# A recurrent unit's gate products as three fp32r passes, with inputs and weights split channel by channel

## The reference, cut to what matters

```python
def rg_lru(u, w_rg, b_rg, w_ig, b_ig, lru_lambda):
    ...
    ub = uf.reshape(B, S, LRU_BLOCKS, LRU_BLOCK_DIM)
    r = jax.nn.sigmoid(jnp.einsum('bshi,hij->bshj', ub, w_rg).reshape(B, S, LRU_WIDTH) + b_rg)
    i = jax.nn.sigmoid(jnp.einsum('bshi,hij->bshj', ub, w_ig).reshape(B, S, LRU_WIDTH) + b_ig)
    ...
    log_a = -LRU_C * r * jax.nn.softplus(-lru_lambda)
    a = jnp.exp(log_a)
    xin = jnp.sqrt(-jnp.expm1(2.0 * log_a)) * (i * uf)
    ...
    _, h = lax.associative_scan(combine, (a, xin), axis=1)
```

## Time and profile before

| | us |
|---|---|
| median of 3 runs | 2747.89 |
| lowest, highest | 2747.36, 2748.41 |
| the profiled execution, its own time | 2748.5 |
| span of that execution | 2746.7 |
| TensorE busy in it | 2711.8 (99%) |
| ScalarE, VectorE, GpSimd busy | 1533.2, 1812.7, 1052.8 |
| mean granted TensorE clock | 0.998 |

### The profile page before, as it was taken

How to read it: one execution, slowest core, us unless ns; L and a number is a source line. 1 busy time by engine, 2 the same in 40 slices (tenths; PEclk the granted TensorE clock), 3 DMA queues, 4 the chain that set the end, 5 groups by cost and what they waited for, 6 DMA issues and landing times.

```text
span 2746.7 us, 35684 instructions
## 1 busy us (share of the span) xinstructions
PE 2711.8 (99%) x12846; PEld 2230.5 (81%) x12846; DVE 1812.7 (66%) x1963; ACT 1533.2 (56%) x1959; POOL 1052.8 (38%) x508
## 2 busy tenths in 40 slices
PE   7999999999999999999999999999999999999999
PEld 6887888668888888888888887997877888888887
DVE  8972114888888888888888897724544444444462
ACT  5231004467777777777777775426576644445321
POOL 0012232032222222222222332747888855555530
PEclk9999999999999999999999999999999999999999
DMA  5021114499999999999999993522222333346541
GB/s 170 24 77 39 39 54 155 176 383 410 399 383 383 383 383 382 383 382 383 382 382 383 381 349 150 194 88 100 108 90 100 130 112 128 123 134 201 199 184 62
DMA packets 168684, 615.81 MB, mean 224 GB/s; under 512 B 21201, under 2 KB 47841, under 8 KB 135553
## 3 DMA queue, kind: packets, MB, share of 16 engines
q1 hardware_dynamic: 162528, 592.18, 57.1%
q0 software_dynamic: 5616, 21.12, 2.7%
q10 hardware_dynamic: 434, 1.08, 0.1%
HBM read 551.30 MB, written 61.97 MB: 223 GB/s over the span
## 4 chain that ended last, share of the span: by engine, by line
PE 93%; DVE 5%; ACT 1%; issue 1%; DMA 0%; DVEq 0%; SPq 0%; ACTq 0%
PE bank L1772 24%; PE bank L1440 20%; PE bank L1441 20%; PE bank L1442 20%; PE bank L1786 2%; PE bank L1919 1%; PE bank L1942 1%; PE bank L1909 1%; PE bank L1930 1%; PE bank L1836 0%; PE bank L1795 0%; DVE heT_lo L3136 0%; ACT heT_hi L2337 0%; DVE buffer L3059 0%; DVE buffer L3060 0%
## 5 line engine op out<-in xcount | busy, mean ns | idle before, releaser
L3089 DVE TENSOR_TENSOR slots_lo<-buffer,slots_hi 128x2048 fp32r<-128x2048 f32 x383 | 849.3, 2287 | 101.6 <-ACT slots_hi L2291 101.6
L2291 ACT ACTIVATE slots_hi<-buffer 128x2048 fp32r<-128x2048 f32 x384 | 709.3, 1950 | 45.1 <-PE bank L1772 25.4
L1317 POOL DMA_INDIRECT xacc<-buffer x15 | 276.4, 18426 | 600.0 <-ACT buffer L2361 600.0
L1358 POOL TENSOR_TENSOR w_lo_set<-buffer,w_hi 128x512 fp32r<-128x512 f32 x210 | 302.3, 1469 | 131.9 <-ACT w_hi L2426 130.3
L1772 PE MATMUL bank<-slots_hi,xsT_hi 128*128 128x512 f32 x960 | 256.8, 389 | 1.5 <-DVE xsT_lo L3107 1.3
L1772 PE MATMUL bank<-slots_lo,xsT_hi 128*128 128x512 f32 x960 | 256.6, 389 | 0.0
L1772 PE MATMUL bank<-slots_hi,xsT_lo 128*128 128x512 f32 x960 | 256.6, 389 | 0.0
L1772 PEld LDWEIGHTS bank<-slots_hi,xsT_hi 128*128 128x128 f32 x960 | 180.0, 188 | 39.4 <-issue 1.6
L1772 PEld LDWEIGHTS bank<-slots_lo,xsT_hi 128*128 128x128 f32 x960 | 180.2, 188 | 37.5
L1772 PEld LDWEIGHTS bank<-slots_hi,xsT_lo 128*128 128x128 f32 x960 | 180.2, 188 | 37.4
L1440 PE MATMUL bank<-slots_hi,heT_hi 128*128 128x512 f32 x512 | 202.4, 395 | 3.1 <-DVE heT_lo L3136 3.1
(11 more groups left out here) (538 smaller groups left out, 5636.8 us busy)
## 6 DMA issues: line engine op xcount, KB each, us to landing
buffer<-in_w_gate SPq DMA_DIRECT2D x128, 1024.0 KB, 7.8
buffer<-in_w_up SPq DMA_DIRECT2D x128, 1024.0 KB, 4.8
buffer<-in_w_down SPq DMA_DIRECT2D x128, 1024.0 KB, 8.0
buffer<-in_wstream SPq DMA_DIRECT2D x152, 512.0 KB, 4.2
gd<-buffer SPq DMA_DIRECT2D x28, 512.0 KB, 3.9
buffer<-gd SPq DMA_DIRECT2D x20, 512.0 KB, 7.6
buffer<-in_x SPq DMA_DIRECT2D x16, 512.0 KB, 8.3
od<-buffer SPq DMA_DIRECT2D x48, 130.0 KB, 2.0
```

What stands on the lines that cost most here:

```text
L1317: nc.gpsimd.indirect_dma_start(out=xacc, out_offset=bass.IndirectOffsetOnAxis(ap=idx_scatter, axis=0), in_=ys, in_offset=None, compute_op= ...
L1358: nc.gpsimd.tensor_tensor(lo, chunk_raw[p % 2][i], hi.bitcast(F32), ALU.subtract).then_inc(chunk_split.sem, 1)
L2291: fn(slots_hi[:, n_ % NH, :], slots[n_ % NS], ACT.Copy).then_inc(slot_high_ready, 1)
L3089: tt2(slots_lo[:, place_of(n_), :], slots[n_ % NS], slots_hi[:, n_ % NH, :].bitcast(F32), ALU.subtract).then_inc(slot_split, 1)
```

## The change

- Each gate product becomes three fp32r passes (L1909): high weight by high input, high weight by low input, low weight by high input. Twelve matmuls a channel stand in place of four.
- Four steps are added to the list. `gate_high` (offset 1, ScalarE) copies the channel's gate weights of 128x256 to a high part; `gate_low` (offset 2, VectorE) makes their low part. `uc_high` (offset 4, ScalarE) copies the convolved input of 128x1024; `uc_low` (offset 4, VectorE) makes its low part. The input's parts lie in the buffers `ra` and `ii`, which the gates' results fill later, so `uc_high` waits for the scan of the channel before, and ScalarE's `gate` waits until both products of a half are made.
- All steps from `gate` on move one count later: gate 5 to 6, mix 7 to 8, gated 9 to 10, root 10 to 11, gatedin 11 to 12, scan 12 to 13.
- TensorE's `gate` waits for the two low parts instead of `uc`.
- The gate weights of channels 0 to 3 are still loaded ahead, in one transfer; the other two transfers go. Those of channel c+4 (128 KB) are loaded by SyncE at the event `scan` of channel c, behind the store of the scan's result.

The diff, cut, engine by engine. The list of steps and the places of the parts:

```diff
-CHANNEL_STEPS = (("tap0", 0), ("tap1", 1), ("tap2", 2), ("tap3", 3), ("gate", 5), ("mix", 7), ("gated", 9), ("root", 10),
-                 ("gatedin", 11), ("scan", 12))
+CHANNEL_STEPS = (("tap0", 0), ("tap1", 1), ("gate_high", 1), ("tap2", 2), ("gate_low", 2), ("tap3", 3), ("uc_high", 4),
+                 ("uc_low", 4), ("gate", 6), ("mix", 8), ("gated", 10), ("root", 11), ("gatedin", 12), ("scan", 13))
...
+        uc_hi, uc_lo = part("uc_hi", 9 * K, SEQ), part("uc_lo", 11 * K, SEQ)
```

SyncE, ahead of the stage, and at the event `scan`:

```diff
-            load_gates(2, 6)
...
-            load_gates(0, 0)
+            load_gates(0, 4)
...
-            load_gates(1, 4)
...
                     scanned.wait(sp, c + 1)
                     sp.dma_start(hsd[c], th).then_inc(hs_stored.sem, 16)
+                    if c < 4:
+                        rgig_loaded.wait(sp, 16 * (c + 1))
+                        load_gates(c + 4, 1)
```

TensorE, at the event `gate`:

```diff
-                    pe.wait_ge(uc_ready, c + 1)
-                    rgig_loaded.wait(pe, 48)
+                    rgig_split.wait(pe, c + 1)
+                    uc_split.wait(pe, c + 1)
                     for h in range(2):
+                        hs = slice(h * HALF, (h + 1) * HALF)
                         for name, j in (("lr", 0), ("li", 1)):
                             bank = b2.wait_free(pe, (name, c, h))
-                            mm(bank[:], rgig[c][:, j, :], uc[:, h * HALF:(h + 1) * HALF],
-                               start=True, stop=True).then_inc(full2, 1)
+                            mm(bank[:], rgig_hi[c % 4][:, j, :], uc_hi[:, hs], start=True, stop=False)
+                            mm(bank[:], rgig_hi[c % 4][:, j, :], uc_lo[:, hs], start=False, stop=False)
+                            mm(bank[:], rgig_lo[:, c % 4, j, :], uc_hi[:, hs], start=False, stop=True).then_inc(full2, 1)
```

ScalarE:

```diff
                 elif kind == "gate":
                     c = event[1]
-                    scanned.wait(act, c)
                     for h in range(2):
                         hs = slice(h * HALF, (h + 1) * HALF)
-                        bank = b2.wait_full(act, ("lr", c, h))
+                        b2.wait_full(act, ("li", c, h))
+                        bank = b2.bank(("lr", c, h))
...
+                elif kind == "gate_high":
+                    c = event[1]
+                    rgig_loaded.wait(act, 16 * max(1, c - 2))
+                    fn(rgig_hi[c % 4], rgig_raw[:, c % 4], ACT.Copy).then_inc(rgig_high_ready.sem, 1)
+                elif kind == "uc_high":
+                    c = event[1]
+                    act.wait_ge(uc_ready, c + 1)
+                    scanned.wait(act, c)
+                    fn(uc_hi, uc, ACT.Copy).then_inc(uc_high_ready.sem, 1)
```

VectorE:

```diff
+                elif kind == "gate_low":
+                    c = event[1]
+                    rgig_high_ready.wait(dve, c + 1)
+                    tt2(rgig_lo[:, c % 4], rgig_raw[:, c % 4], rgig_hi[c % 4].bitcast(F32), ALU.subtract).then_inc(rgig_split.sem, 1)
+                elif kind == "uc_low":
+                    c = event[1]
+                    uc_high_ready.wait(dve, c + 1)
+                    tt2(uc_lo, uc, uc_hi.bitcast(F32), ALU.subtract).then_inc(uc_split.sem, 1)
```

More of the change, by code:

```diff
@@ L483, in build_program @@
         merged2_lo4 = part("merged2_lo4", 0, 4, SEQ)
+        rgig_lo = part("rgig_lo", 52176, 4, 2, P)
+        rgig_hi_pairs = [part("rgig_hi0", 3584, 2, 2, P), part("rgig_hi1", 7680, 2, 2, P)]
+        rgig_hi = [rgig_hi_pairs[c // 2][:, c % 2] for c in range(4)]
+        uc_hi, uc_lo = part("uc_hi", 9 * K, SEQ), part("uc_lo", 11 * K, SEQ)
         psum = [ctx.enter_context(nc.psum_tensor(f"bank{i}", [P, HALF], F32)) for i in range(8)]
@@ L628, in build_program @@
         uc, ra, th, ii = [at((8 + i) * K, SEQ) for i in range(4)]
-        rgig_parts = [at(52176, 4, 2, P), at(3584, 2, 2, P), at(7680, 2, 2, P)]
-        rgig = [rgig_parts[0 if c < 4 else c // 2 - 1][:, c if c < 4 else c % 2] for c in range(8)]
+        rgig_raw = at(52176, 4, 2, P)
         y_pair, Kh = at(8 * K, 2, HALF), at(10 * K, 2, SEQ)
@@ L798, in build_program @@
         d_ready, w_ready, O_scaled = sem("d_ready"), sem("w_ready"), sem("O_scaled")
+        rgig_high_ready, rgig_split = Later(sa_ready, 4 * NE), Later(he_ready, 4 * NE)
+        uc_high_ready, uc_split = Later(heT_high_ready, 4 * NE), Later(heT_ready, 4 * NE)
         lru_s_ready, uc_ready, lru_to_act, act_to_lru = (sem("lru_s_ready"), sem("uc_ready"), sem("lru_to_act"),
@@ L1047, in load_weights, with load_gates @@
                                  a["wstream"][I_PAIR + 2 * p + f]).then_inc(w_loaded[p % 2].sem, 16)
-            def load_gates(i, c):
-                sp.dma_start(rgig_parts[i].rearrange("p a b c -> p (a b c)"),
-                             a["rgig"][:, 256 * c:256 * c + (1024 if i == 0 else 512)]).then_inc(rgig_loaded.sem, 16)
+            def load_gates(c, n):
+                sp.dma_start(rgig_raw[:, c % 4:c % 4 + n].rearrange("p a b c -> p (a b c)"),
+                             a["rgig"][:, 256 * c:256 * (c + n)]).then_inc(rgig_loaded.sem, 16)
             def load_late(n):
```

## The result

| | before, us | after, us |
|---|---|---|
| median of 5 runs each | 2747.89 | 2759.83 |
| lowest, highest | 2747.36, 2749.25 | 2759.07, 2762.46 |
| the profiled execution, its own time | 2748.5 | 2759.67 |
| span of that execution | 2746.7 | 2757.5 |
| TensorE busy in it | 2711.8 | 2711.4 |

After against before is 1.0044, 95% interval 1.0033 to 1.0055: the change makes the kernel slower by 11.9 us. The forecast was 2750.4 with a range up to 2758; the time lies 1.8 above that range.

The account below looks back on a forecast made before the run. TensorE, busy 99% of the span, was taken to bound the kernel. Saved 5.9 us against gate waits of 8.4 gave net +2.5 on the median 2747.9, so 2750.4 us, range 2743 to 2758.

Parts of the forecast that it names:

- The saving: At each gate, twelve fp32r matmuls take 2.72 us instead of 3.45, saving 0.73 a channel, 5.9 for eight.
- The place of the loss: TensorE waits for `uc_low` at the gates: 1.35 us in channels 1 to 4, 1.0 in 5 to 7, none at 0.
- The row of five steps: Scan, SyncE's issues, weights' landing and GpSimd's sums, second copy and `uc_high`, then `uc_low`; lets TensorE start at 17.67, not 16.32.
- The edits costed at nothing: Other added steps, later gate results, `root`, exchange chunks and the two removed transfers were taken to cost 0 us.
- step 3: Raw weights land 4.63 us behind their issue, at 6.78; GpSimd's four sums then take 7.13, ending at 13.91.
- the rival of the longer wait: Weights' packets start after the store's: 1.85 us more a channel, waits 20.9 in sum, 2762.9 us; chance 0.16.

Follow-up runs that it names:

- the two kernels with the split first: The changed kernel with `uc_high` one count earlier, ahead of ScalarE's chunk copies, once alone (2742.51 us) and once also with the scan back at count 12 (2743.88 us).
- scan at 12: Against the changed kernel, the scan is back at count 12, ahead of the sixth product's post-add; 2745.20 us, 0.9987 of before.
- first experiment: Against the changed kernel, SyncE issues the raw weights ahead of the scan's store and the gate weights; 2749.21 us, 1.0004 of before.
- fifth experiment: Against the first experiment, the store and gate weights wait for the third product of the next pair; 2745.64 us, 0.9985 of before.
- second experiment: Against the changed kernel, only the 128 KB of gate weights go behind the raw weights, the store stays ahead; 2755.36 us, 1.0026 of before.
- input split first: Against the changed kernel, `uc_high` moves from offset 4 to 3, ahead of ScalarE's chunk copies; 2742.51 us, 0.9979 of before.
- weights first: The first experiment: raw weights issued ahead of the store and gate weights, against the changed kernel; 2749.21 us.
- store apart: The fifth experiment: store and gate weights held until the next pair's third product, against weights first; 2745.64 us.
- fourth experiment: Input split first: `uc_high` ahead of ScalarE's chunk copies, against the changed kernel; 2742.51 us.
- third experiment: Scan at 12: the scan back at its old count, against the changed kernel; 2745.20 us.
- The kernel with both edits: Against the changed kernel, `uc_high` at offset 3 and the scan back at count 12 together; 2743.88 us, 0.9979 of before.

## Why the prediction was wrong

**What held.** The saving: channel 0's gate, without a wait, takes 1871.15 to 1873.91 = 2.76 us for twelve matmuls against 3.45, where 2.72 was forecast, and the two kernels with the split first, without waits, are faster by 5.8 to 5.9. The place of the loss: TensorE waits at the gates of channels 1 to 7, behind `uc_low`, not at channel 0's and not at a product. The row of five steps: store and gate weights ahead of the raw weights, GpSimd's first sum held by that transfer, `uc_high` behind the second copy. The edits costed at nothing cost nothing: in those two kernels the whole saving appears.

**What failed: step 3, the landing of the weights.** Times from the pair's start, channel 2:

| | forecast | after |
|---|---|---|
| scan ends | 1.47 | 0.66 |
| weights issued | 2.15 | 1.78 |
| weights landed (behind their issue) | 6.78 (4.63) | 8.28 (6.50) |
| sums end (length) | 13.91 (7.13) | 14.60 (6.27) |
| `uc_high` ends | 15.62 | 16.23 |
| TensorE's gate | 17.67 | 18.40 |

I took the landing from a row in which the store had gone out 2.90 ahead, and stores land after 2.6, so that nothing else of this row of steps was under way. In after the seven channels' landings are 7.08, 6.50, 6.78, 6.39 with gate weights ahead and 6.07, 5.95, 6.36 without. Two smaller errors went the other way and hid part of it: the scan took 2.50 instead of 3.27, and the sums, starting later, had mostly passed the taps, so one of them was slowed (2.15) where two had been. A third added to it: SyncE's two issues took 1.10 where I had 0.66. The waits came to 13.6 instead of 8.4. That the forecast came this close is partly luck. The seven landings exceed 4.63 by 12.7 in sum, so by an estimate from these rows the landing that I assumed would have left waits of about 0.9 in all, not 8.4.

The waits alone don't carry the time out of the range: 2747.9 - 5.9 + 13.6 = 2755.6, and 2757.3 with the clock. The last 2.5 us up to the median of 2759.8 are not explained by the stage; in the profiled execution 1.6 of it arose ahead of it, and the rest stays open.

The prediction had this case, as the rival of the longer wait, with 1.85 us more for the landing; measured are 1.87 at channel 2 and 1.3 to 2.5 over the seven. That price came out, but from a mechanism that doesn't hold, so it is luck; and its waits of 20.9 in sum and its 2762.9 were too high, because the two smaller errors took part of the price back. It spoke of packets that only start when the store's are through, and held against it that "a store and a load may overlap". Loads that are issued ahead of the store are slowed as well, so the store needn't be through; being under way together is what costs. The trace of before had two signs that I passed over. The stores `gd`, which go out two at a time, have a median of 3.9 from issue to landing, against 2.6 for the single store. And ahead of channel 6's gate, where channel 5's store led by 2.33, the landing took 5.39 (SyncE's list, then ScalarE's first copy, of before):

```profile
2100.30 0.33 SPq L1162 DMA_DIRECT2D hsd<-buffer  x1
2102.63 1.39 SPq L1046 DMA_DIRECT2D buffer<-in_wstream  x2
```

```profile
2108.02 0.63 ACT L2426 ACTIVATE w_hi<-buffer 128x512 fp32r<-128x512 f32 x1 [2.06 <-DMA buffer<-in_wstream]
```

There the two issues took 1.39 instead of 0.81; in after they take 1.07 to 1.33. So 0.3 to 0.5 us of after's long landings may lie in the issues themselves; no run separates that. The store's lead alone doesn't explain this row: in scan at 12 the store leads by 2.00 to 2.23, and the landings of channels 2, 4 and 6 take 4.68, 4.79 and 4.52.

The Trainium skill's page "DMA: Bandwidth & Descriptors" (section Queues, rings and completion order), which the prediction cited, says that each DMA engine takes a queue's descriptors in the order of its ring, though a later one may finish its write earlier. Read as a rule for what must wait for what, it would have the weights of the first experiment land as if alone, at 4.5; they took 5.7 to 6.3. The same page (section Issuing engines are not separate DMA queues) says that transfers run on the same 16 DMA engines and interleave with each other, whichever engine started them; all of these are SyncE's, and the first and the fifth experiment (5.7 to 6.3 against 4.5) agree with interleaving.

**What was not foreseen.** The fall of the clock behind one wait, 1.7 us; the prediction had no term for it. And TensorE reached channel 0's gate at 1871.15, where 1866.80 + 2.72 = 1869.52 was due: 1.6 us from ahead of the stage. In the six experiments that gate starts between 1867.84 and 1870.82, so executions spread by this much, and I don't put it down to the change.

**The sum again**, on the profiled executions: +2.5 forecast, +5.2 waits, +1.7 clock, +1.6 ahead of the stage = 11.0; measured are 2759.67 - 2748.5 = 11.2.

## What to carry to other kernels

A duration from issue to landing belongs to the company in which it was measured: when a change moves a transfer next to others, add their time to it whichever is issued first, and look through all rows of before for the ones in which they stood closest. When a step is moved one place later on a list, write down what the queue behind it will then carry together. Where a small step hangs behind a copy that waits for a transfer, first ask whether it has to stand there; moving `uc_high` ahead of the copies was worth more here, by the medians, than anything done to the transfers.

## What the runs showed of the hardware

- **A store slows the loads beside it on one queue, whichever is issued first.** Two weight loads of 512 KB take 4.4 to 4.8 us from issue to the first use alone or with the store at least 2.0 ahead (but 5.39 in the one row of before), and 5.7 to 6.4 with a store of 512 KB issued right ahead or right behind (but 7.61 in one row of the second experiment). With 128 KB more ahead they take 6.4 to 7.1 in after; in input split first the rows spread from at most 5.75 to 8.04. The store pays as well, and for it the order does count: its median from issue to landing is 2.6 in before, 3.0 in after, where the weights follow it, and 6.3 where the weights go first. Apart from the weights it is 4.4; there half of the stores go out right behind the two of `gd` (groups of DMA issues of after, weights first and store apart):

```profile
hsd<-buffer SPq DMA_DIRECT2D x8, 512.0 KB, 3.0
```

```profile
hsd<-buffer SPq DMA_DIRECT2D x8, 512.0 KB, 6.3
```

```profile
hsd<-buffer SPq DMA_DIRECT2D x8, 512.0 KB, 4.4
```

- **The clock can fall behind a wait of 2 us in a stage in which TensorE is otherwise busy without a break.** It fell behind an idle time of 1.92 at channel 2 of after and 2.27 at channel 1 of the second experiment, and not behind 2.22 and 1.96 at channels 1 and 3 of after. The length of the wait alone doesn't decide; what does is open.
- **VectorE and GpSimd.** `uc_low` takes 1.23 in the fourth experiment, where it starts at 1947.87, 0.11 ahead of a sum of GpSimd that then takes 2.26 instead of 1.29. In after it starts while GpSimd is at its low parts and takes 2.04 itself. The Trainium skill's "SBUF — State Buffer" (section SBUF: two separate sides) says that whichever of the two starts first holds their common port for the whole instruction; these rows agree.
- **The scan's length hangs on GpSimd too.** Its mean is 3264 ns in before, 2586 in after and 2291 with the scan back at its old count. Where it starts ahead of a subtraction of GpSimd it takes 2.29, and the subtraction then takes 3.09; where it starts behind one that is running, it takes 2.50 to 3.27. GpSimd's row beside the scan of the earlier trace rows, then a scan of the third experiment and GpSimd's row beside it:

```profile
1929.25 2.16 POOL L1358 TENSOR_TENSOR w_lo_set<-buffer,w_hi 128x512 fp32r<-128x512 f32 x1
```

```profile
1929.80 2.29 DVE L3366 TENSOR_TENSOR_SCAN buffer<-buffer 128x1024 f32<-128x1024 f32 x1
```

```profile
1930.09 3.09 POOL L1364 TENSOR_TENSOR w_lo_set<-buffer,w_hi 128x512 fp32r<-128x512 f32 x1 [1.40 <-ACT w_hi L2434]
```

  The kernel with both edits has the two cases side by side: seven of its scans take 2.29, and the one that starts at 2137.62, 0.21 behind a subtraction of GpSimd, takes 3.27.
